# Other address distances between the operands of TensorE's matmuls, by the order of allocation alone

## What is computed

```python
h = rmsnorm(x, norm1_g); parts = split(h @ w_in)          # w_in 1024 x about 13300
y = three scans (hgrn2, mlstm, ssd), each normed and gated
x = x + (sum of gate_b * (y_b @ w_br_b)) @ w_out           # three 1024 x 1024, then one
x = x + conv_ffn(rmsnorm(x, norm2_g), w_up, w_down)        # 1024 x 5632, 2816 x 1024
x = rmsnorm(x, final_g)
for i in range(2):                                         # second block, two layers
    z, zc = mod(rms_norm(x)) @ w_in[i], mod(rms_norm(ctx)) @ w_in[i]   # 1024 x 2048
    x = x + g1 * (attention and gating of z, zc) @ w_out[i]
    x = x + g2 * conv_ffn(mod(rms_norm(x)), w_up[i], w_down[i])
    if i == 0: the same two steps for ctx (256 more tokens)
return x
```

## Time and profile before

| what | value |
|---|---|
| median of three executions | 1674.22 us (1673.27 to 1677.38) |
| the profiled execution's own time | 1668.64 us |
| its span, first to last instruction | 1666.9 us |
| mean granted clock of TensorE in it | 0.993 of full speed |

### The profile page before, as it was taken

One profiled execution on the slowest core, in us unless ns is written; L12 is line 12 of the kernel. 1 busy time (PEld: TensorE's weight loads), 2 busy tenths in 40 slices (PEclk: granted clock), 3 DMA queues, 4 the chain that ended last, 5 costly groups with the idle time before them and its releaser, 6 DMA issues.

```text
span 1666.9 us, 34323 instructions
## 1 busy us (share of the span) xinstructions
PE 1615.7 (97%) x14687; PEld 1444.3 (87%) x14687; DVE 1213.5 (73%) x2054; ACT 877.3 (53%) x1335; POOL 199.5 (12%) x124
## 2 busy tenths in 40 slices
PE   8999999999999999999989999999999998899999
PEld 7999888898999999997757888888877786699999
DVE  3374499587777886587766888877888778568864
ACT  4435645548546665446675543323433456666653
POOL 4303540000000110100000111110110100041100
PEclk9999999999999999999999999999999999999999
DMA  7656555354455555521102234463344323045544
GB/s 278 243 217 226 200 219 187 153 228 174 136 189 186 196 180 170 188 98 65 52 2 102 94 135 155 158 209 147 127 170 171 133 77 102 2 160 199 199 164 140
DMA packets 41128, 259.65 MB, mean 156 GB/s; under 512 B 4368, under 2 KB 7696, under 8 KB 14480
## 3 DMA queue, kind: packets, MB, share of 16 engines
q1 hardware_dynamic: 40976, 257.46, 43.3%
HBM read 256.39 MB, written 1.05 MB: 154 GB/s over the span
## 4 chain that ended last, share of the span: by engine, by line
PE 77%; DVE 16%; ACT 3%; DMA 2%; issue 2%; SPq 0%; DVEq 0%; ACTq 0%
PE acc_psum L197 23%; PE acc_psum L199 22%; PE acc_psum L198 22%; DVE w_low_sb L163 3%; PE acc_psum L2511 2%; PE acc_psum L206 2%; DVE mod_products L324 2%; PE acc_psum L2537 1%; DVE ring_sb L324 1%; DVE u_filtered L2064 1%; PE acc_psum L260 1%; DMA ring_sb<-in_w_up 1%; ACT w_high_sb L152 1%; ACT norm_rt_sb L2761 1%; PE acc_psum L1098 1%
## 5 line engine op out<-in xcount | busy, mean ns | idle before, releaser
L197 PE MATMUL acc_psum<-h_high_sb,w_high_sb 128*128 128x256 f32 (+1 forms) x2176 | 657.5, 302 | 4.9 <-DVE h_low_sb L486 2.6
L199 PE MATMUL acc_psum<-h_high_sb,w_low_sb 128*128 128x256 f32 (+1 forms) x2176 | 648.8, 298 | 0.0
L198 PE MATMUL acc_psum<-h_low_sb,w_high_sb 128*128 128x256 f32 (+1 forms) x2176 | 647.8, 298 | 0.0
L152 ACT ACTIVATE w_high_sb<-ring_sb 128x1024 fp32r<-128x1024 f32 (+2 forms) x412 | 386.9, 989 | 369.5 <-PE acc_psum L199 221.7
L163 DVE TENSOR_TENSOR w_low_sb<-ring_sb,w_high_sb 128x1024 fp32r<-128x1024 f32 (+1 forms) x358 | 391.1, 1135 | 109.5 <-ACT w_high_sb L152 100.0
L197 PEld LDWEIGHTS acc_psum<-h_high_sb,w_high_sb 128*128 128x128 f32 x2176 | 409.3, 188 | 32.0 <-issue 12.6
L199 PEld LDWEIGHTS acc_psum<-h_high_sb,w_low_sb 128*128 128x128 f32 x2176 | 409.4, 188 | 16.5
L198 PEld LDWEIGHTS acc_psum<-h_low_sb,w_high_sb 128*128 128x128 f32 x2176 | 409.2, 188 | 16.5 <-issue 0.5
L163 POOL TENSOR_TENSOR w_low_sb<-ring_sb,w_high_sb 128x1024 fp32r<-128x1024 f32 x54 | 132.2, 2472 | 671.8 <-ACT w_high_sb L152 671.7
L2064 DVE SCALAR_TENSOR_TENSOR u_filtered<-acc_psum,par_sb,u_filtered 128x255 f32<-128x255 f32 (+2 forms) x264 | 150.7, 571 | 43.8 <-ACT u_filtered L2201 24.0
L197 PE MATMUL acc_psum<-u_high,w_high_sb 128*128 128x256 f32 (+1 forms) x528 | 168.6, 319 | 4.4 <-DVE w_low_sb L163 3.0
(11 more groups left out here) (312 smaller groups left out, 1869.1 us busy)
## 6 DMA issues: line engine op xcount, KB each, us to landing
ring_sb<-in_w_in SPq DMA_DIRECT2D x68, 1024.0 KB, 6.4
ring_sb<-in_w_up SPq DMA_DIRECT2D x66, 1024.0 KB, 4.9
ring_sb<-in_w_down SPq DMA_DIRECT2D x48, 704.0 KB, 4.1
ring_sb<-in_w_ada SPq DMA_DIRECT2D x24, 1024.0 KB, 4.8
ring_sb<-in_w_ada_rows SPq DMA_DIRECT2D x24, 1024.0 KB, 5.0
ring_sb<-in_w_out SPq DMA_DIRECT2D x12, 1024.0 KB, 4.9
ring_sb<-in_w_br_hg SPq DMA_DIRECT2D x4, 1024.0 KB, 6.8
ring_sb<-in_w_br_ml SPq DMA_DIRECT2D x4, 1024.0 KB, 5.0
```

The source lines that it names most:

```text
L152: self.nc.scalar.activation(self.high[:, g % 2, piece], self.ring[:, c % RING, piece], ACT.Copy)\
L197: nc.tensor.matmul(out, sh, mh, start=start, stop=False)
L198: nc.tensor.matmul(out, sh, ml, start=False, stop=False)
L199: return nc.tensor.matmul(out, sl, mh, start=False, stop=stop)
```

## The change

The two small tensors `first_gain` and `first_weight` (32 bytes each) are allocated between the ring and `w_high` instead of between X and H. Between X and H stand `select` (96 bytes) and `lam` (272 bytes, rounded up to 288) instead of them and `mod_gains` (128 bytes), which goes to the place at the end where `lam` was. No instruction is added, taken away or moved.

```diff
@@ Core.__init__
         self.ring = self.sbuf("ring", [P, RING, SLOT])
+        self.first_gain, self.first_weight = (self.sbuf(n, [P, DT])[:, :] for n in ("first_gain", "first_weight"))
         self.loaded = [self.sig(f"weights_loaded_{i}") for i in range(RING)]
 
         self.high, self.low = (self.sbuf(n, [P, 2, SLOT], F32R) for n in ("w_high", "w_low"))
@@ build
         X = sb("X", [P, DT, 2 * S])
-        core.first_gain, core.first_weight = (sb(n, [P, DT])[:, :] for n in ("first_gain", "first_weight"))
-        core.mod_gains = sb("mod_gains", [P, 2, DT, 2])
+        select = sb("select", [P, Modulation.ROWS])
+        core.lam = sb("lam", [P, 4 + 64])
         H = tuple(sb(n, [P, DT, 2 * S], F32R) for n in ("h_high", "h_low"))
@@
         mod_sums = core.mod_sums = sb("mod_sums", [P, 2, UNIT])
-        select = sb("select", [P, Modulation.ROWS])
         small = sb("small", [P, 64])
         core.gate_columns = sb("gate_columns", [P, ST, 3, MB_H])
-        core.lam = sb("lam", [P, 4 + 64])
+        core.mod_gains = sb("mod_gains", [P, 2, DT, 2])
```

## The result

The changed kernel takes 1693.07 us in the median (1692.13 to 1695.10, four executions) beside 1674.99 us for the kernel before (1673.27 to 1677.38, four on the same chip): ratio 1.0117, 95% interval 1.0093 to 1.0140. That is 18 us slower. The forecast was 19 us faster. The profiled execution of the changed kernel took 1693.36 us, its span is 1691.6 us.

What follows compares the result with a forecast made beforehand. TensorE's matmul pace was taken as the bound: 18.7 us from slow 256-column steps plus 3.7 us at 512 columns, 22.4 x 0.84 = 18.9 us, so 1674.2 - 18.9 = 1655 us, range 1650 to 1685.

Steps and rivals of the forecast that it cites:

- What bounds the kernel: TensorE is busy 97% of the span, so the change can act only through the pace of the matmuls of `product`.
- two paces for one shape: Matmuls of 256 columns start 113.3 ns apart in quick stretches and 117.8 ns in slow ones.
- the working of the distances: From w_high, the change takes H's distance from 64 to 256 and u's from 64 to 0, modulo 512 bytes.
- What does a distance other than 64 do?: For product matmuls, u at 0 and H at 256 were both taken to run at the quick pace.
- a picture of where the reads meet: Geometry argument for H: 256 is the farthest apart two starts can be in a 512-byte period; given no more than half.
- The bound above is the slow pace throughout, and possibly a slower one: Upper limit for H at distance 256, for which the profile had no row; the quick pace was taken instead.
- The sum: Gains on product matmuls at both widths, 22.4 x 0.84 = 18.9 us off 1674.2, giving 1655 us.
- The share of 0.84: Part of product matmul time on the end's path: 1117 us of 1323 us.
- (b): 256 is a bad place: H loses its quick steps, u at 0 gains; net 10.4 us slower, 1685 us; chance 0.22.
- (a): Distance decides nothing, only how a stream restarts does; about 1674 us, between 1669 and 1679; chance 0.25.
- (c): Only one helps: u at 0 alone 1670 us, H at 256 alone 1660 us; chance 0.13 in all.
- The fourth part: VectorE's and ScalarE's splits, with ring to w_high going from 24576 to 24640 bytes, were costed at nothing.

Runs made afterwards that it cites:

- run a: Kernel before with 64 bytes put ahead of w_high, everything behind moving along, both distances still 64 modulo 512; 1677.21 us, ratio 1.0008.
- b: Kernel before with only H moved to distance 256, w_high in its place and u still at 64; 1693.44 us, ratio 1.0099.
- run c: Kernel before with only u moved to distance 0, w_high and H as they were; 1680.18 us, ratio 1.0021.
- run d: Computation replaced by streams of float32r matmuls only, at 16 distances from 0 to 480 bytes; at 256 columns 120.0 ns a step at 0, 113.3 at 192.
- run f: Kernel before with H and u both moved to distance 96; 1696.39 us, ratio 1.0121.
- h: Matmul streams only, four distances, ten restarts, also narrower weight loads; at 256 columns all ten 120.0 ns at 0, seven 113.3 and three 117.7 at 192.
- e: Kernel before with H at distance 192, u at 192 in 256-column sections and 0 in the 512-column one; 1669.1 us, ratio 0.9955.
- j: Run e repeated unchanged; 1669.27 us, ratio 0.9963.

## Why the prediction was wrong

*What bounds the kernel* held: the time moved with the pace of L197 to L199 and with nothing else. So did the reading that there are two paces for one shape, that a pace holds until an interruption, that other engines don't set it, and the working of the distances: run a shows that a new place with the old distance does not bring the 120.0 ns, and runs b and c that it is H's distance and u's. One reading was off: it took all three kinds to stand at 64, but counted as moving less stationary the distance with the weights moving was 192.

*The step that failed* is "What does a distance other than 64 do?", in both halves. For 0, I took a row of 512 columns for u, of which two thirds of the matmuls have 256. The row was right for its width, since u in run c steps at 226.7 ns too; at 256 columns 0 gives 120.0, which run c and run d show. For 256 there was no row. I took a picture of where the reads meet, and the picture had the wrong period: 256 and 0 are the same distance. "The bound above is the slow pace throughout, and possibly a slower one" named the right side, but the sum of the rivals then used 117.8 and not more.

*The sum* with the measured steps: the settled steps at 256 columns go from 115.7 ns in the mean to 119.8, and 7.8 thousand times 4.1 is 32 us. The 1680 at 512 columns go from 228.9 to 226.8 and give back 3.5 us. That is 28 us, and TensorE's busy time grew by 28.1. The share of 0.84 makes it 24, and the span grew by 24.7. So the share was right for the whole, and the term's size and sign were not. It is right only as a mean over the stages: in the up sections all of the loss reaches the end (6.7 of 6.7 us each), and in the 512-column stage run f gives 6.0 of 11. Against the median the loss is less; the likely reason is that executions before hold on average more slow steps than the profiled one.

*The rivals.* (b) came nearest: slower, with H at 256 in a state from which no restart leads out. It named the right operand, but its reason, that 256 is a worse place than 0, is refuted by runs c and d. Its price was short (10.4 us of 18), because the pace is a third one, and because it let u gain at 0, where run c shows a loss of 0.2%. At 512 columns it had H lose, and H gained there. (a) is refuted by runs b and c. In (c), u at 0 helps at 512 columns alone.

*The fourth part* (splits by VectorE and ScalarE) held: 1221 and 1051 ns, and run a gives no difference.

In run d the moving tensor stays in its place, and the place of the weights alone takes the step at 256 columns from 113.3 to 120.0 ns. The Trainium skill ("TensorE: Matmul & The Clock Gate", Part 2, Step-by-step) says that loading the next weights takes nothing from the running matmul. The float32r streams here do not bear that out.

What stays open is the mechanism under the table of run d: why the extra comes in these sizes, why the two widths differ, and which phase a restart takes. Open too is the second pace at 512 columns in run a. A clash of two reads of the same memory would fit a pace that hangs on both operands' places, but was only argued.

## What to carry to other kernels

Where a stream of float32r matmuls bounds the kernel, read the step between starts, not the busy share, and sort it by shape: two paces for one shape point at something outside the program's order. The distance between the starts of the moving and the stationary operand, modulo 256 bytes, is then worth a row of short streams on the chip before it is tuned in the kernel, and each width has to be measured for itself (here 192 for 256 columns, 0 for 512). A price taken from a row of another shape is not a price, and three restarts are too few to call a pace the only one.

## What was not expected of the hardware

- The period of 256 bytes was new, and so was a pace (120.0 ns at 256 columns) that is slower than both of the kernel before. Distance 0 gave it in the changed kernel, in runs b and c and in every stream of runs d and h. Distances 64 and 192 have two paces each (113.3 and 117.8 ns), and which one holds can change at a restart.
- At 512 columns the order turns round: 0 is best with 226.7 ns, 64 has 228.9 (and 233.3 in run a alone), and all others lie between 232.3 and 234.2.
- Allocation alone moved this kernel from 1669 us (runs e and j) to 1696 us (run f), with the same instructions in the same order.
- The kernel before spreads over 17 us between executions, the changed one over 3 us in four. A stream with two paces would look like noise from outside; that this is the cause of the spread is argued and not shown.
